# Roots of the mean squares: a row made by products with the identity, or by a store to DRAM and a load back

## The chip, the core and the metric

The program runs on one core of a Trainium2 chip. Such a core has five engines that each run their own list of instructions in order and wait for one another through semaphores: TensorE (PE, matrix products; its weight loads are listed as PEld), VectorE (DVE), ScalarE (ACT), GpSimd (POOL) and SyncE (SP), which here only issues DMAs. The metric is the device time of one execution in microseconds, the median of some runs. Profile times are from one profiled execution.

## The reference

The reference is two blocks of two layers each on one sequence of 256 tokens with 1024 channels, all in float32. Each layer is a feed-forward part, a mixer (attention of several kinds in the first block; a state-space scan and latent attention in the second), and a second feed-forward part. So there are eight feed-forward parts and four mixers, one after the other. What the change touches is the norm ahead of a feed-forward part:

```
def rmsnorm(x, g):
    xf = x.astype(jnp.float32)
    y = xf * lax.rsqrt(jnp.mean(xf * xf, axis=-1, keepdims=True) + EPS)
    return y.astype(x.dtype) * g

def swiglu(h, w_gate, w_up, w_down):
    return (jax.nn.silu(h @ w_gate) * (h @ w_up)) @ w_down

x = x + 0.5 * swiglu(rmsnorm(x, g), w_gate, w_up, w_down)      # w_gate, w_up: 1024 x 2816; w_down: 2816 x 1024
```

The root `rsqrt(...)` is one number for each token, 256 in all. As it scales whole rows of `x`, the kernel multiplies with the gains `g` first, does the products with `w_gate` and `w_up` on the unscaled rows, and scales the results by the roots afterwards.

## The kernel before

**Phases.** `PHASES` lists twelve phases; `T0[p]` is the number of the first weight tile of phase p. A feed-forward phase (`tensor_ffn`, `scalar_ffn`, `vector_ffn`) goes over 33 weight tiles of 1 MB: gate tile i and up tile i in turn for i = 0 to 10 (steps s = 0 to 21), then 11 tiles of `w_down`. Step s works on tile `T0[p] + s`.

**A weight tile's way.** SyncE loads it into one of three buffers `ST` (`load_tile`, L153 in the profile). ScalarE copies it to `WH` in the reduced precision fp32r (`weights_hi`, L117), VectorE takes the remainder `WL = ST - WH` (`weights_lo`, L120), and TensorE multiplies with both, so that a product has nearly the precision of float32. ScalarE and VectorE prepare tile `T0[p] + s + 2` in step s. SyncE loads tile i once VectorE has done with tile i - 3, which is in the same buffer. SyncE's list is written tile by tile in `sync_program`: small loads are placed behind a given tile's load, and whatever one of them waits for holds back all loads after it.

**A gate or up tile on TensorE.** For each of 8 slices k of the 1024 channels there are two products with `WH` (moving 512 columns, the high and low part of X beside each other) and two with `WL` (256 columns). The results lie the other way round from X: channels of the hidden layer are on the partitions, the 256 tokens are along the free axis. The four halves of the product for a gate tile use PSUM banks 4 and 5, those of an up tile 6 and 7. Before TensorE starts the next tile of the same kind, VectorE must have read the banks: ScalarE copies one half to `EB` and VectorE adds it to the other (`gate_sum` writes `GS` for a gate tile; the sum of an up tile goes to `HQ`, shown as `H`).

**The roots.** ScalarE squares and sums the rows of X (`rms`), and takes the square root; VectorE inverts it in step 1 (`rms_end`, the RECIPROCAL of L138), which gives `RR`, two columns of 128 partitions (`RR` is a part of the tile `SM`, and is shown as `SM`). In `RR` a token is a partition, but for the products a token is a position along the free axis, the same on all partitions. So a row `RBC` of 256 roots is wanted in each of the 128 partitions. `r_row`, after the products of step 2, makes it on TensorE: two float32 products of the identity (`ident`, a part of `C`) with one column of `RR` repeated 128 times, into bank 3. `row_end` copies the bank to `RBC` on VectorE at the end of its step 2. In step 3 VectorE multiplies `GS` by `RBC` (name `gg`), ScalarE takes its silu, and then VectorE multiplies `HQ` by `RBC` (`scale_up`) and by `GS`. These two products with `RBC` occur for each of the 11 pairs of tiles of a phase; the row is made once in a phase, and first used in step 3, ahead of the sum of gate tile 1 (`gate_sum`) that frees banks 4 and 5 for step 4.

The second block's mixers (`mix2`) also make a row with `r_row` and `row_end`.

Of the kernel before, what the change touches and what calls it, by code (L numbers as in the profile page):

```python
# [5 lines left out]
F32 = mybir.dt.float32  # L6
# [6 lines left out]
T, DM, DF = 256, 1024, 2816  # L13
# [327 lines left out]
def build(nc, I, consts, out, phases=PHASES):  # L341
# [3 lines left out]
    def sem(name):  # L345
        return ctx.enter_context(nc.semaphore(name))
# [11 lines left out]
    def at(*name):  # L358

        return known[name] if known else (PE.sem, 1)  # L360
# [21 lines left out]
    def ar(name, shape, off, dt=F32):  # L382
        return sb(name, shape, dt, ARENA + off)
# [62 lines left out]
    WS, DCOL, BROW = ar("WS", [128, 32], D0 + 512), ar("DCOL", [128, 16], D0 + 640), ar("BROW", [128, 3, 32], D0 + 704)  # L446
    QKR = ar("QKR", [128, 2, 64], D0 + 1088)
    AHT = ar("AHT", [32, T], D0 + 1600)
    SCR = nc.dram_tensor("decay", (2, 32, T), F32, kind="Internal").ap()
    CB = ar("CB", [128, 2, 2, 260], 80896)  # L450
    QNT, QRT = sb("QNT", [128, 2, 2, T], F32R, R2), sb("QRT", [128, 2, 2, T], F32R, R2 + 16384)
# [119 lines left out]
    s_gain, s_x = sem("gains_landed"), [sem("x0_landed"), sem("x1_landed")]  # L571
    s_ident, s_const, s_out = sem("ident_landed"), sem("const_landed"), sem("out_stored")
    s_par = [sem(f"par{l}_landed") for l in range(2)]
    s_scr = [sem(f"decay{l}_stored") for l in range(2)]
    s_dec = [[sem(f"decay{l}_half{n}_landed") for n in range(8)] for l in range(2)]
    landed, rounds = {}, [0] * NS
# [104 lines left out]
    def r_row(e, p, b):  # L681
        clear(b)
        e.wait_ge(*at("rr", p))
        for t in range(2):
            m = e.matmul(PS[:, b, of(t)], RR[:, t:t + 1].to_broadcast([128, 128]), ident, True, True)
        m.then_inc(*e.done("rrow", p))
        freed[b] = ("rbc", p)
# [22 lines left out]
    def tensor_ffn(e, p):  # L710
        begun = set()
        for s, (what, i) in enumerate(FFN):
            tile = T0[p] + s
            wh, wl = view(WH, tile), view(WL, tile)
            if tile not in CUT:
                e.wait_ge(*at("lo", tile))
            if what == "d":
                if i < NP - 2:
                    for name, a, kind, c in EIGHT if i in PLAIN else SEVEN:
                        ends = i == SUMMED[-1] and name in ("m1", "m5", "m6", "m7")  # L720
                        m = tensor_product(e, p, i, name, a, kind, c, begun, ends)
                        if ends:
                            m.then_inc(*e.done(name, p))
                    m.then_inc(*e.done("tile", tile))
                elif i == NP - 2:
                    freed.update({0: ("um", p), 1: ("x", p, 1, 1), 2: ("x", p, 0, 1), 3: ("x", p, 1, 0), 4: ("x5", p),
                                  5: ("x7", p), 6: ("um", p), 7: ("x", p, 0, 0)})
                    for group in ("m2", "m3", "c22", "m4"):
                        own = [(j, r) for j in (i, i + 1) for r in (EIGHT if j in PLAIN else SEVEN) if r[0] == group]
                        for j, (name, a, kind, c) in own:  # L730
                            if (group, j, c) == ("m4", i + 1, 1):
                                m.then_inc(*e.done("tile", tile))
                                if p + 1 < len(phases):
                                    turn_x(e, p + 1, "", 0)
                            m = tensor_product(e, p, j, name, a, kind, c, begun, (j, (name, a, kind, c)) == own[-1])
                        m.then_inc(*e.done(group, p))
                    e.also("tile", tile + 1)
                continue
            if p == 0 and s == 18:
                e.wait_ge(s_const, NCONSTS)  # L740
                for gi in range(1, 4):
                    turn_gains(e, gi, gi - 1)
            b = 4 + 2 * (what == "u")
            clear(b, b + 1)
            for k in range(8):
                if s == 0 and k == 3:
                    turn_x(e, p, "", 1)
                if tile in CUT:
                    e.wait_ge(*at("lo", tile, k * CUT[tile] // 8))
                if s == 0:  # L750
                    e.wait_ge(*at("xl", p, "", k))
                for f in range(2):
                    e.matmul(PS[:, b + f, :], wh[:, k, of(f)], XHL[:, k, :, :].rearrange("p a t -> p (a t)"), k == 0, False)
                for f in range(2):
                    m = e.matmul(PS[:, b + f, 0:256], wl[:, k, of(f)], XH[:, k, :], False, k == 7)
            m.then_inc(*e.done("tile", tile))
            freed[b] = freed[b + 1] = ("us" if what == "u" else "gs", p, i)
            if s == 2:
                r_row(e, p, 3)

    def wide(e, tile, hi, lo, ks, banks, first, last, cols, off=0):

# [873 lines left out]
    def row_end(e, p, b):  # L1636
        e.wait_ge(*at("rrow", p))
        e.wait_ge(*e.last())
        e.tensor_copy(RBC[:, :], PS[:, b, 0:256]).then_inc(*e.done("rbc", p))
# [66 lines left out]
    def scale_up(e, p, i):  # L1706

        h = HQ[i].rearrange("p (k t) -> p k t", k=2)
        e.wait_ge(*at("us", p, i))
        e.wait_ge(*at("rbc", p))  # L1710
        e.tensor_tensor(h, h, RBC[:, :].unsqueeze(1).to_broadcast([128, 2, T]), ALU.mult).then_inc(*e.done("un", p, i))

    def pair_sums(e, p, i):
# [37 lines left out]
    def vector_ffn(e, p):  # L1751
        t0 = T0[p]
        for s in range(len(FFN)):
            for i in range(NP):
                if s == UP_AT[i] + 1:
                    e.wait_ge(*at("ub", p, i))
                    e.tensor_tensor(HQ[i], PS[:, 6:8, 0:256], EB[:, :, :], ALU.add).then_inc(*e.done("us", p, i))
                if s == max(UP_AT[i] + 1, 3):
                    e.wait_ge(*at("rbc", p))
                    e.wait_ge(*at("gs", p, i))  # L1760
                    e.tensor_tensor(GS[i % 2], GS[i % 2], RBC[:, :].unsqueeze(1).to_broadcast([128, 2, T]),
                                    ALU.mult).then_inc(*e.done("gg", p, i))
                if s == GATE_AT[i] + 1 and (p or i):
                    gate_sum(e, p, i)
# [11 lines left out]
                tile_sums(e, p, s + 2 - DOWN)  # L1776
            if s == 1:
                rms_end(e, p)
            if s == 2:
                row_end(e, p, 3)  # L1780
            for i in range(NP):
                if s == HIDDEN_AT[i]:
                    e.wait_ge(*at("silu", p, i))
# [718 lines left out]
    def load_params(e, l):  # L2502
        for j, name in enumerate(("dt_bias_2", "a_log_2", "d_skip_2")):
            e.dma_start(BROW[:, j, :], I[name][l].unsqueeze(0).to_broadcast([128, 32])).then_inc(s_par[l], 16)
        for j, name in enumerate(("q_norm_2", "k_norm_2")):
            e.dma_start(QKR[:, j, :], I[name][l, 128:192].unsqueeze(0).to_broadcast([128, 64])).then_inc(s_par[l], 16)

    def load_decay(e, p, l, n):

        i = n  # L2510
        if n == 0:
            e.wait_ge(*at("ahl", p))
            e.dma_start(SCR[l], AHT[:, :]).then_inc(s_scr[l], 16)
            e.wait_ge(s_scr[l], 16)
            e.wait_ge(*at("ol", p, 7))
        if n == 2:
            e.wait_ge(*at("tile", T0[p] + MIX2T.index(("mla", 1)) + 1))
        if n > 3:
            e.wait_ge(*at("yo", p, 2 * HAD[n] + 1))
        e.dma_start(ME[i].rearrange("p h c t -> p (h c t)"), SCR[l, 4 * n:4 * n + 4, :].rearrange("h t -> (h t)").unsqueeze(0)  # L2520
                    .to_broadcast([128, 4 * T])).then_inc(s_dec[l][n], 16)
        for h in range(2):
            e.dma_start(EA[i][64 * h:64 * h + 64, :, :], SCR[l, 4 * n + h:4 * n + 4:2, 128:256].unsqueeze(0)
                        .to_broadcast([64, 2, 128])).then_inc(s_dec[l][n], 16)

    def sync_program(e):
        load_x(e, 0)
        e.dma_start(C[:, 0:128], consts[:, 0:128]).then_inc(s_ident, 16)
        load_rows(e, 0, *groups[0][0], s_gain)
        for j in range(CUT[0]):  # L2530
            load_part(e, 0, j)
            if j == 1:
                load_x(e, 1)
        for j in range(CUT[1]):
            load_part(e, 1, j)
        load_tile(e, 2)
        for i in range(NS, NT):
            load_tile(e, i)
            for j in range(2 * (i - NS), 2 * (i - NS) + 2):
                if j < NCONSTS // 16:  # L2540
                    load_const(e, j)
            for p, (kind, l, _) in enumerate(phases):
                if kind == "mix2" and i == T0[p] + 4:
                    e.wait_ge(*at("x", p - 1, 0, 1))
                    load_params(e, l)
                for n in range(8):
                    if kind == "mix2" and i == T0[p] + (30, 30, 35, 35, 36, 37, 40, 42)[n]:
                        load_decay(e, p, l, n)
        p = len(phases) - 1
        for t, n in ((1, 1), (1, 0), (0, 0), (0, 1)):  # L2550
            e.wait_ge(*at("x", p, t, n))
            e.dma_start(out[0, of(t), half(n)], X[:, t, half(n)]).then_inc(s_out, 16)
        e.wait_ge(s_out, 64)
# [63 lines left out]
```

## Time and profile before

| | |
|---|---|
| median of 3 runs | 2609.53 us (2609.23 to 2610.02) |
| profiled execution | 2610.11 us, of which 2608.3 us are the span from the first to the last instruction |
| TensorE matmul | busy 2593.6 us, 99% of the span, 14500 records |
| VectorE | busy 2080.4 us, 80% |
| ScalarE | busy 1550.4 us, 59% |
| DMA | 471.89 MB, queue 1 busy for 54.5% of 16 engines' span |
| TensorE's granted clock | 1.00 of full speed, the mean of the core |

A row of a timeline gives the start, the duration, the engine, the line, the operation with its output and input tiles, and the number of merged instructions; in brackets stands how long the engine sat idle before it, and who released it. The line is often that of a helper (L111 is any matmul, L120 any VectorE operation on two tensors, L153 any DMA), so the tile names tell the groups apart. Records of matmuls overlap: an instruction is pipelined behind the one ahead of it, and the distance between two starts is what it costs. A float32 product leaves two records in the trace.

### The profile page before, as it was taken

To read this page: it belongs to the slowest core of one execution; us is meant where nothing else is said; L and a number is where in the kernel's file an instruction comes from. 1 tells how busy PE (TensorE), PEld (TensorE's weight loads), DVE (VectorE), ACT (ScalarE), POOL (GpSimd) and SP (SyncE) were. 2 spreads that over 40 slices of the span, in tenths; PEclk is the share of its full clock that TensorE was granted. 3 is DMA by queue.
4 is the path that set the end of the run, shared out by engine and by line. 5 is a ranking of instruction groups with operands and counts; after the bars stand their busy time and mean duration, and the time that the engine had idled before them with its cause. 6 is when DMAs were issued, how large, how long until landed. Compare 5 with 4: busy or idle time off the path is not lost.

```text
span 2608.3 us, 35583 instructions
## 1 busy us (share of the span) xinstructions
PE 2593.6 (99%) x14500; PEld 2223.6 (85%) x14500; DVE 2080.4 (80%) x2647; ACT 1550.4 (59%) x2014; POOL 286.6 (11%) x254
## 2 busy tenths in 40 slices
PE   9999999999999999999999999999999999999999
PEld 7888788888888888888889998888888899988887
DVE  7897767887886767887888878678878888786788
ACT  6546665546556665545557767455455577674553
POOL 0003210000004110000003123200000031232000
PEclk9999999999999999999999999999999999999999
DMA  7554445555555445555555465555555564645553
GB/s 252 179 199 162 162 162 183 188 193 190 183 181 185 147 172 182 192 179 194 183 184 188 133 212 161 187 184 188 184 194 179 185 188 136 211 161 183 188 186 137
DMA packets 342752, 471.89 MB, mean 181 GB/s; under 512 B 18810, under 2 KB 259516, under 8 KB 342588
## 3 DMA queue, kind: packets, MB, share of 16 engines
q1 hardware_dynamic: 342588, 469.61, 54.5%
q8 instruction: 114, 1.87, 0.3%
q14 instruction: 50, 0.41, 0.0%
HBM read 468.46 MB, written 1.11 MB: 180 GB/s over the span
## 4 chain that ended last, share of the span: by engine, by line
PE 97%; DVE 1%; ACT 1%; issue 0%; DMA 0%; SPq 0%; DVEq 0%
PE PS L111 95%; PE PS L114 3%; DVE WL L120 1%; ACT WH L117 0%; ACT XHL L117 0%; DVE SB L125 0%; DMA ST<-in_ffn_w_gate 0%; DVE XB L128 0%; DVE H L120 0%; DVE ANG L125 0%; DVE ANG L128 0%; DVE XHL L128 0%; DVE SB L131 0%; ACT KV L117 0%; SPq L153 0%
## 5 line engine op out<-in xcount | busy, mean ns | idle before, releaser
L120 DVE TENSOR_TENSOR WL<-ST,WH 128x2048 fp32r<-128x2048 f32 (+3 forms) x442 | 988.4, 2236 | 209.2 <-ACT WH L117 205.4
L111 PE MATMUL PS<-XHL,WH 128*128 128x512 f32 (+1 forms) x4096 | 1123.5, 362 | 3.7 <-DVE XHL L128 2.3
L117 ACT ACTIVATE WH<-ST 128x2048 fp32r<-128x2048 f32 (+3 forms) x442 | 817.4, 1852 | 291.5 <-PE PS L111 285.4
L111 PEld LDWEIGHTS PS<-XHL,WL 128*128 128x128 f32 x3456 | 652.2, 189 | 125.3
L111 PE MATMUL PS<-XHL,WL 128*128 128x256 f32 x3456 | 735.1, 279 | 0.0
L111 PEld LDWEIGHTS PS<-XHL,WH 128*128 128x128 f32 x4096 | 629.2, 190 | 8.3 <-DVE XHL L128 3.3
L111 PE MATMUL PS<-WH,XHL 128*128 128x512 f32 (+3 forms) x1472 | 460.4, 387 | 0.0
L117 ACT ACTIVATE EB<-PS 128x512 f32<-128x512 f32 x176 | 105.3, 598 | 415.7 <-PE PS L111 412.6
L111 PEld LDWEIGHTS PS<-WH,XHL 128*128 128x128 f32 x1472 | 273.7, 188 | 58.2 <-issue 6.8
L111 PE MATMUL PS<-WL,XHL 128*128 128x512 f32 (+3 forms) x736 | 280.5, 381 | 0.0
L111 PE MATMUL PS<-WH,HH 128*128 128x512 f32 x544 | 215.1, 395 | 0.0
L111 PE MATMUL PS<-WH,HL 128*128 128x512 f32 x544 | 214.9, 395 | 0.0
L111 PE MATMUL PS<-WL,HH 128*128 128x512 f32 x544 | 214.0, 393 | 0.0
L120 POOL TENSOR_TENSOR X<-X,TS 128x512 f32<-128x512 f32 x8 | 14.4, 1797 | 1590.1 <-DVE TS L128 1590.1
L111 PEld LDWEIGHTS PS<-WL,XHL 128*128 128x128 f32 x736 | 138.5, 188 | 24.8 <-issue 1.0
L111 PE MATMUL PS<-WH,RH 128*128 128x512 f32 (+1 forms) x352 | 135.2, 384 | 1.2 <-ACT KV L117 1.2
L111 PE MATMUL PS<-WL,RH 128*128 128x512 f32 (+1 forms) x352 | 133.7, 380 | 0.0
L111 PE MATMUL PS<-WH,RL 128*128 128x512 f32 (+1 forms) x352 | 133.7, 380 | 0.0
L120 DVE TENSOR_TENSOR H<-PS,EB 128x512 f32<-128x512 f32 x88 | 60.8, 691 | 91.1 <-ACT EB L117 91.0
L111 PEld LDWEIGHTS PS<-WH,HL 128*128 128x128 f32 x544 | 102.1, 188 | 24.3
L111 PEld LDWEIGHTS PS<-WL,HH 128*128 128x128 f32 x544 | 102.1, 188 | 23.9
L111 PEld LDWEIGHTS PS<-WH,HH 128*128 128x128 f32 x544 | 102.2, 188 | 23.1
(274 smaller groups left out, 2954.6 us busy)
## 6 DMA issues: line engine op xcount, KB each, us to landing
ST<-in_ffn_w SPq DMA_DIRECT2D x132, 1024.0 KB, 4.9
ST<-in_w_in SPq DMA_DIRECT2D x106, 1024.0 KB, 5.1
ST<-in_ffn_w_down SPq DMA_DIRECT2D x44, 1024.0 KB, 4.9
ST<-in_ffn_w_gate SPq DMA_DIRECT2D x43, 1024.0 KB, 5.2
ST<-in_ffn_w_up SPq DMA_DIRECT2D x43, 1024.0 KB, 5.1
ST<-in_w_ssd_out SPq DMA_DIRECT2D x16, 1024.0 KB, 5.0
ST<-in_w_branch SPq DMA_DIRECT2D x8, 1024.0 KB, 5.0
ST<-in_w_out SPq DMA_DIRECT2D x8, 1024.0 KB, 5.1
```

The source lines that it names most:

```text
L111: return self.eng.matmul(o, l, r, start=start, stop=stop) if self.eng else Said()
L114: return self.eng.transpose(o, v, ident) if self.eng else Said()
L117: return self.eng.activation(o, v, f, **kw) if self.eng else Said()
L120: return self.eng.tensor_tensor(o, a, b, op) if self.eng else Said()
```

## The change

Only the eight feed-forward phases change. TensorE no longer runs `r_row` there, VectorE no longer runs `row_end`, and SyncE gets a new function `spread_roots`, placed directly behind the load of tile `T0[p] + 5`. It waits for the reciprocal `rr`, stores the two columns of `RR` to a DRAM tensor `ROOTS` (128 words of 4 bytes each), waits until both have landed, and loads the 256 words as a row into all 128 partitions of `RBC` (1 KB each). The two uses of `RBC` wait for the semaphore `s_row` of that load. The mixers keep their products with the identity.

```
+    ROOTS = nc.dram_tensor("roots", (len(phases), 2, 128), F32, kind="Internal").ap()
...
+    s_root, s_row = sem("roots_stored"), sem("roots_landed")
+
+    NTH = {p: sum(k == "ffn" for k, _, _ in phases[:p + 1]) for p in range(len(phases)) if phases[p][0] == "ffn"}
...
             freed[b] = freed[b + 1] = ("us" if what == "u" else "gs", p, i)
-            if s == 2:
-                r_row(e, p, 3)
...
         e.wait_ge(*at("us", p, i))
-        e.wait_ge(*at("rbc", p))
+        e.wait_ge(s_row, 16 * NTH[p])
...
                 if s == max(UP_AT[i] + 1, 3):
-                    e.wait_ge(*at("rbc", p))
+                    e.wait_ge(s_row, 16 * NTH[p])
...
-            if s == 2:
-                row_end(e, p, 3)
...
+    def spread_roots(e, p):
+
+        e.wait_ge(*at("rr", p))
+        for t in range(2):
+            e.dma_start(ROOTS[p, t].unsqueeze(1), RR[:, t:t + 1]).then_inc(s_root, 16)
+        e.wait_ge(s_root, 32 * NTH[p])
+        e.dma_start(RBC[:, :], ROOTS[p].rearrange("t p -> (t p)").unsqueeze(0).to_broadcast([128, T])).then_inc(s_row, 16)
...
+                if kind == "ffn" and i == T0[p] + 5:
+                    spread_roots(e, p)
```

TensorE, between step 2 and step 3 of a feed-forward phase (here the second such phase; the six others and the first read alike). `PS<-XHL,WH` and `PS<-XHL,WL` are the products of a tile, `PS<-C,SM` those with the identity:

```order
 L111 MATMUL PS<-XHL,WH 128x512 x2
 L111 MATMUL PS<-XHL,WL 128x256 x2
-L111 MATMUL PS<-C,SM 128x128 [waits dve_done]
-L111 MATMUL PS<-C,SM 128x128
 L111 MATMUL PS<-XHL,WH 128x512 [waits dve_done]
 L111 MATMUL PS<-XHL,WH 128x512
```

Two float32 products and one wait are gone, and nothing else moves on TensorE.

VectorE, at the end of step 2 and in step 3 of the same phase (`GS_73` is the buffer of gate tile 0, `GS_74` that of gate tile 1, `H_0_76` that of up tile 0):

```order
 L120 TENSOR_TENSOR H_0_76<-PS,EB 128x512 [waits act_done]
 L120 TENSOR_TENSOR WL<-ST,WH 128x2048 [waits act_done]
-L135 COPY RBC<-PS 128x256 [waits dve_done,pe_done]
-L120 TENSOR_TENSOR GS_73<-GS_73,RBC 128x512 [waits dve_done]
+L120 TENSOR_TENSOR GS_73<-GS_73,RBC 128x512 [waits roots_landed]
 L120 TENSOR_TENSOR GS_74<-PS,EB 128x512 [waits dve_done,act_done]
 L120 TENSOR_TENSOR WL<-ST,WH 128x2048 [waits act_done]
```

The copy is gone with its wait for TensorE; the first product with `RBC` now waits for a DMA, with the sum of gate tile 1 behind it.

SyncE, in the changed kernel, from the load of tile `T0[p] + 4` of the same phase on (`roots<-SM` are the stores, `RBC<-roots` is the load of the row; before, the five loads of `ST` follow one another):

```order
L153 DMA ST<-in_ffn_w_gate 128x8x256 [waits dve_done]
L153 DMA ST<-in_ffn_w_up 128x8x256 [waits dve_done]
L153 DMA roots<-SM 128x1 [waits dve_done]
L153 DMA roots<-SM 128x1
L153 DMA RBC<-roots 128x256 [waits roots_stored]
L153 DMA ST<-in_ffn_w_gate 128x8x256
L153 DMA ST<-in_ffn_w_up 128x8x256 [waits dve_done]
L153 DMA ST<-in_ffn_w_gate 128x8x256 [waits dve_done]
```

The load of tile `T0[p] + 6` now stands behind two waits: for the reciprocal and for the landing of the stores.

## Rows read from the trace of the kernel before

**Rows 1.** The page's busy times and the chain that ended last.
```profile
PE 2593.6 (99%) x14500; PEld 2223.6 (85%) x14500; DVE 2080.4 (80%) x2647; ACT 1550.4 (59%) x2014; POOL 286.6 (11%) x254
...
PE 97%; DVE 1%; ACT 1%; issue 0%; DMA 0%; SPq 0%; DVEq 0%
```

**Rows 2.** Timeline of TensorE around the row's products, the phase at 411 us.
```profile
424.58 0.63 PE L111 MATMUL PS<-XHL,WH 128*128 128x512 f32 x2
...
425.27 0.61 PE L111 MATMUL PS<-C,SM 128*128 128x128 f32 x4
425.64 0.71 PE L111 MATMUL PS<-XHL,WH 128*128 128x512 f32 x2
...
426.42 0.63 PE L111 MATMUL PS<-XHL,WH 128*128 128x512 f32 x2
...
431.30 0.63 PE L111 MATMUL PS<-XHL,WH 128*128 128x512 f32 x2
```

**Rows 3.** Instructions of tile SM: the row's products; ns min/median/max, first and last start.
```profile
L111 PE MATMUL PS<-C,SM x40: 270/275/275, 28.3 to 2440.4; 128*128 128x128 f32 x40
```

**Rows 4.** Timeline of VectorE, same phase, steps 1 to 3.
```profile
420.51 0.17 DVE L138 RECIPROCAL SM<-SM 128x2 f32<-128x2 f32 x1
...
422.33 2.29 DVE L120 TENSOR_TENSOR WL<-ST,WH 128x2048 fp32r<-128x2048 f32 x1 [0.86 <-ACT WH L117]
425.92 0.42 DVE L135 COPY RBC<-PS 128x256 f32<-128x256 f32 x1 [1.29 <-PE PS L111]
426.38 0.69 DVE L120 TENSOR_TENSOR GS<-GS,RBC 128x512 f32<-128x512 f32 x1
427.18 0.69 DVE L120 TENSOR_TENSOR GS<-PS,EB 128x512 f32<-128x512 f32 x1
```

**Rows 5.** Timeline of SyncE's queue, same phase.
```profile
414.56 0.37 SPq L153 DMA_DIRECT2D ST<-in_ffn_w_up  x1
420.50 0.37 SPq L153 DMA_DIRECT2D ST<-in_ffn_w_gate  x1
424.65 0.37 SPq L153 DMA_DIRECT2D ST<-in_ffn_w_up  x1
```

**Rows 6.** DMA issues: KB each, median us to landing.
```profile
ST<-in_ffn_w_up SPq DMA_DIRECT2D x43, 1024.0 KB, 5.1
...
out<-X SPq DMA_DIRECT2D x4, 256.0 KB, 2.1
...
QKR<-in_k_norm SPq DMA_DIRECT2D x2, 32.0 KB, 5.2
decay<-AHT SPq DMA_DIRECT2D x2, 32.0 KB, 5.2
```

**Rows 7.** Timeline of SyncE's queue: two DMAs of one word for each partition.
```profile
61.99 1.06 SPq L153 DMA_DIRECT2D POS<-in_positions  x2
```

**Rows 8.** SyncE's waits: us in total, times, longest.
```profile
SPq L153 <- DMA decay<-AHT: 9.2, 2, 4.8
```

**Rows 9.** Timeline of ScalarE and VectorE, same phase: tile 6 is split.
```profile
431.99 1.91 ACT L117 ACTIVATE WH<-ST 128x2048 fp32r<-128x2048 f32 x1
...
433.93 2.29 DVE L120 TENSOR_TENSOR WL<-ST,WH 128x2048 fp32r<-128x2048 f32 x1 [0.52 <-ACT WH L117]
...
437.07 0.60 ACT L117 ACTIVATE EB<-PS 128x512 f32<-128x512 f32 x1 [2.66 <-PE PS L111]
...
442.64 0.60 ACT L117 ACTIVATE EB<-PS 128x512 f32<-128x512 f32 x1 [2.65 <-PE PS L111]
```

**Rows 10.** Timeline of TensorE and VectorE in the first phase.
```profile
25.66 0.17 DVE L138 RECIPROCAL SM<-SM 128x2 f32<-128x2 f32 x1 [1.37 <-ACT SM L117]
...
27.96 2.29 DVE L120 TENSOR_TENSOR WL<-ST,WH 128x2048 fp32r<-128x2048 f32 x1 [1.12 <-ACT WH L117]
...
28.67 0.70 PE L111 MATMUL PS<-XHL,WH 128*128 128x512 f32 x2
```

**Rows 11.** Waits, 103 to 130 us: total us, times, longest.
```profile
PE PS L111 <- DVE GS L120: 1.4, 1, 1.4
```

## The prediction, made before the changed kernel was run

> **What bounds the kernel now.** I read the page's busy times and its chain of waits first. TensorE is busy for 99% of the span, and 97% of the chain that ended last is its own work [rows 1]. So a microsecond taken out of TensorE's list is a microsecond gained, and a microsecond added elsewhere costs nothing until TensorE waits for it. The second view is TensorE's timeline around the two products that go. The start of each record there follows the one before at an even pace and no idle time is shown: TensorE doesn't wait at this place [rows 2]. The third is VectorE's timeline: it does wait, 1.29 us, for TensorE to reach the row's products, and copies the row afterwards [rows 4]. The fourth and fifth are the queue of SyncE and the DMAs' landing times [rows 5, 6], as the new work goes there.
>
> **What goes on TensorE.** A slice k of a tile begins every 0.70 us: from the WH pair at 425.64 one would expect the next at 426.34, but it starts at 426.42 since the row's products still occupy the array. From the WH pair at 424.58 to that at 426.42 there are 1.84 us, in which two slices take 1.39 (a slice at 0.70: the copies to EB after steps 4 and 5 are 442.64 - 437.07 = 5.57 apart, eight slices). The row costs 1.84 - 1.39 = 0.45 us [rows 2, 9]. The trace has 40 records of these products, four to a row: ten rows, of which two are the mixers' and stay [rows 3]. At the seven other feed-forward phases the same distance is 1.83 or 1.84 us, so eight give 8 x 0.45 = 3.6 us. Nothing else moves on TensorE, and bank 3 is not used again until the tiles of w_down, so the saving is whole.
>
> **What goes on VectorE.** A copy of 0.42 us and the wait of 1.29 us in seven phases [rows 4]. VectorE is not waited for here: the sum of gate tile 1 ends at 427.18 + 0.69 = 427.87, while TensorE wants its banks at 431.30 [rows 2, 4]. I cost this at nothing. What it does is to leave VectorE free at 422.33 + 2.29 = 424.62 for the first product with the row, which stood at 426.38.
>
> **What comes: the row's way.** The roots are there at 420.51 + 0.17 = 420.68 [rows 4]. The trace before shows no store of single words. For the issue, the nearest rows are loads of one word for each partition: two took 1.06 us in the queue [rows 7], 0.53 each, so the second store starts at about 421.2. For a landing, the nearest rows are 2.1 us (256 KB stored from X, with nothing ahead of it) and 5.2 us (the decay rows, 32 KB, issued right behind a 1 MB tile) [rows 6]. Which of them applies is read from the queue: tile 5's load was issued at 414.56 and lands 5.1 us later, at 419.7, and tile 6's now stands behind the stores [rows 5, 6]. The queue is empty, so I take 2.1: landed at 423.3. The row's load is 128 KB from DRAM; between the same 2.1 us and 5.2 us (QKR, a load of 32 KB into all partitions behind a tile) [rows 6] I take 2.2, the lower end for the same reason: landed at 425.6, or 4.9 us after the roots. The product starts 0.8 us earlier than before instead of later. The bounds of the two landings are 2.1 + 2.1 and 5.2 + 5.2.
>
> The Trainium skill, "DMA: Bandwidth & Descriptors", section on the anatomy of one DMA, gives a fixed cost of about 2.0 us for each DMA, most of it the confirmation of the write. By it the row would come at about 425.5, and the sum would be the same. The same section warns that this "can cause a surprisingly long delay especially when the write target is HBM"; the stores of X to the output, at 2.1 us, show no such delay [rows 6], and that of the decay rows has its 1 MB tile ahead of it. What it would do here is rival (a) below.
>
> **How late may the row be?** Behind the waiting product stands the sum that frees banks 4 and 5. From the start of the product to the end of the sum are 427.87 - 426.38 = 1.49 us [rows 4]. TensorE starts step 4 at 431.30 - 0.45 = 430.85 [rows 2], so the row may land until 429.36, which is 8.7 us after the roots. There are 3.8 us to spare. The first phase is tighter, as its square sums come late: roots at 25.83, VectorE free at 30.25, the row by my figures at 25.83 + 4.9 = 30.75, and TensorE's step 4 at 28.67 + 5.66 - 0.45 = 33.88 (5.66 is 431.30 - 425.64), so until 32.39 [rows 2, 10]. 1.6 us to spare there.
>
> **What SyncE's waits hold back.** The stores wait for the roots and the row's load for the stores; the load of tile 6 is behind both. It was issued at 420.50 [rows 5]; now it is at about 423.3 + 0.5 = 423.8, 3.3 us later. It lands at 428.9 to 429.3. ScalarE begins to split it at 431.99, so nothing waits [rows 9]. With more delay it would still have room: WL is done 4.23 us after the start of the split (433.93 + 2.29 - 431.99), and TensorE starts step 6 at about 442.4 - 0.45 = 442.0 (the EB copy of step 5's banks at 442.64 marks it), so the tile may land until 437.7 [rows 9]. Tile 7, wanted from SyncE at 424.65 [rows 5], is issued on time; its bytes queue behind those of tile 6, by some 3 us, and it is split only after the copy to EB at 437.07 [rows 9]. The cost is nothing, and even at 5.2 us for each landing tile 6 would be issued at 427.1 and land at 432.2. In the row of SyncE's waits one sees that such a wait is paid by the queue itself: it stood 4.8 us for the decay store [rows 8].
>
> The Trainium skill states this on the same page and in the same section as a rule: DMA engines do not wait on semaphores, any wait is made by the issuing sequencer. The trace agrees with its 4.8 us.
>
> **Sum.** -3.6 us on TensorE, nothing elsewhere: the profiled execution of 2610.11 us would be 2606.5. The median of the runs shown is 0.6 lower, 2609.53, which gives 2605.9.
>
> **Rivals.**
> (a) The row comes late in every phase, and the kernel gets slower: stores of single words, 4 bytes at a time, are confirmed slowly. For it speaks that no row shows such a store. Each microsecond past 8.7 us from the roots is one on TensorE in each of eight phases. With both landings at 5.2 the row comes at 421.2 + 10.4 + 0.1 = 431.7, 2.3 us late: 8 x 2.3 - 3.6 = +15, or 2624.6. It equals the time before at 9.1 us from the roots, and is 0.2% slower from 9.8. Against it: the empty queue.
>
> (b) Only the first phase is late, where 1.6 us are spare and small loads of constants share the queue: up to 2 us of stall, 2605.9 to 2607.9.
>
> (c) The weight tile is late. This needs SyncE to be held until 432.6, 12 us after the roots; each microsecond more then costs one in each phase, so one past it gives 2605.9 + 8 = 2613.9. Against it: even the upper bounds of (a) don't reach it.
>
> (d) What TensorE saves is given back at a place where it waits for another engine, as 1.4 us at 125 us [rows 11]: 2609.5. Against it: that chain starts from a bank that TensorE filled, so it moves with TensorE.
>
> (e) The saving is larger, since VectorE (80% busy) is relieved too: 0.46 us more in each phase (426.38 - 425.92), 2605.9 - 3.7 = 2602.2. For it speaks VectorE's share, against it that TensorE shows no wait for VectorE in these steps [rows 2].
>
> **Chances.** A measurement of this kernel can tell about 0.2%, 5.2 us, from no change. Forecast 2605.9: 0.78; its own range is 2605.3 to 2606.6 (0.40 to 0.50 us a phase and the spread of the runs). (a) 0.08, of it 0.07 over 5.2 us slower; (b) 0.03; (c) 0.01, slower too; (d) 0.02; (e) 0.08, faster than 0.2%. So faster 0.08, same 0.84, slower 0.08. The forecast's gain itself, 0.14%, falls within the 0.2%. The range 2604.6 to 2609.6 holds the forecast, (b) and (d), and leaves (a), (c) and (e) out.
>
> **What the profile after would show.** TensorE: no records C,SM at the eight places, and 1.39 us for the two slices across the step. VectorE: the first GS<-GS,RBC waits for the DMA of RBC, about 1 us idle, and starts some 4.9 us after the reciprocal. SyncE: the load of tile 6 about 3.3 us after the reciprocal's end, and no wait of ScalarE for ST there. If TensorE has idle time ahead of step 4's first product, (a) is right; ahead of step 6's, (c). The prediction would be wrong if the row takes more than 8.7 us.

## The result, and the profile after

| | before | after |
|---|---|---|
| median, runs | 2609.73 us (2609.23 to 2610.15, 5 runs) | 2667.57 us (2665.91 to 2667.84, 5 runs) |
| ratio | | 1.0219, 95% interval 1.0208 to 1.0230 |
| span of the profiled execution | 2608.3 us | 2665.8 us |
| mean granted clock of TensorE | 1.00 | 0.99 |

The changed kernel is slower by 58 us. The forecast was 2605.9 us, in a range of 2604.6 to 2609.6. Busy times and chain of the page, which answer to [rows 1]:

```profile
PE 2609.0 (98%) x14468; PEld 2234.5 (84%) x14468; DVE 2074.9 (78%) x2639; ACT 1552.8 (58%) x2014; POOL 286.9 (11%) x254
...
PE 90%; DMA 4%; ACT 3%; DVE 2%; issue 0%; SPq 0%; ACTq 0%; DVEq 0%
```

TensorE has 32 records fewer and yet is busy 15.4 us longer, and the span is 57.5 us longer: its idle time grew by 57.5 - 15.4 = 42.1 us. DMAs are now 4% of the chain. The waits of the whole execution (us in total, times, longest) say who it waited for, and who that one waited for:

```profile
DVE GS L120 <- DMA RBC<-roots: 76.9, 8, 11.1
...
PE PS L111 <- DVE GS L120: 42.8, 9, 7.6
```

Eight of the nine waits of TensorE are new; the ninth is that of [rows 11]. "Third phase" here and below is the third of the twelve, which is the second feed-forward phase; before the change it stands at 411 us. There the chain in order of time (start, duration) shows the two steps of the row's way:

```profile
430.40 7.24 DMA roots<-SM
...
437.66 6.30 DMA RBC<-roots
```

Timeline rows of VectorE, SyncE's queue, TensorE and ScalarE in the same stretch, which answer to [rows 2, 4, 5, 9]:

```profile
429.83 0.17 DVE L138 RECIPROCAL SM<-SM 128x2 f32<-128x2 f32 x1
...
430.02 0.82 SPq L153 DMA_DIRECT2D roots<-SM  x2
437.66 0.32 SPq L153 DMA_DIRECT2D RBC<-roots  x1
438.02 0.43 SPq L153 DMA_DIRECT2D ST<-in_ffn_w_gate  x1
...
443.98 0.69 DVE L120 TENSOR_TENSOR GS<-GS,RBC 128x512 f32<-128x512 f32 x1 [10.05 <-DMA RBC<-roots]
444.78 0.69 DVE L120 TENSOR_TENSOR GS<-PS,EB 128x512 f32<-128x512 f32 x1
...
445.62 1.19 PE L111 MATMUL PS<-XHL,WH 128*128 128x512 f32 x2 [5.30 <-DVE GS L120]
...
447.06 1.91 ACT L117 ACTIVATE WH<-ST 128x2048 fp32r<-128x2048 f32 x1 [0.90 <-DMA ST<-in_ffn_w_gate]
```

The roots are there at 430.00, the row at 443.96: 14.0 us where 4.9 were forecast. For most of the stores' 7.2 us no DMA engine moves a byte; the last two figures of this row are the DMA share and GB/s from 432.00 to 437.60:

```profile
432.00:437.60 5.60, 5.60 (x34) 4.86 (x32) 1.93 (x1) 2.80 (x3) 0.00 (x0) 1.00 0.00 0
```

So that time is spent on the confirmation of the writes, not on moving them. TensorE stands for 5.30 us ahead of step 4 until the sum of gate tile 1 has freed its banks. And then it is slow. Three stretches of TensorE (us, busy us and records, granted clock, DMA share, GB/s): the stall, the 6 us behind it, and the next 5.6:

```profile
439.92:445.62 5.70, 0.40 (x4) 0.91 0.62 214
445.62:451.58 5.96, 5.96 (x18) 0.52 0.94 296
451.58:457.20 5.62, 5.62 (x34) 1.00 0.79 241
```

The granted clock was 1.00 while TensorE worked. It fell within the 5.3 us of idle time (mean 0.91 over the stall), and over the next 6 us it is 0.52, that is 0.50 for most of them (1.2 GHz in place of 2.4): 18 records where the next stretch has 34. In the timeline a slice of a tile takes 1.28 us there in place of 0.70.

**The account.** Idle time +42.1 us. Busy time +15.4, which is -3.7 for the products that are gone (TensorE is busy 2589.9 us in the version without stalls, below) and +19.1 that are left for the slow clock, 2.4 a phase. 42.1 - 3.7 + 19.1 = 57.5 us. The clock itself bears the 19.1 out: over the 6.0 us behind each of the eight stalls its mean was 0.74, 0.52, 0.67, 0.56, 0.56, 0.59, 0.59 and 0.72, which makes 6.0 x 3.05 = 18.3 us of lost work, 1.6 to 2.9 in a phase. All eight new waits stand ahead of step 4. They make 41.4 of the 42.1 us, so no more than 0.7 us is idle time anywhere else, ahead of step 6 for one.

### The profile page after: what moved, and what is told of

Its sections match the earlier page's. It is cut to its first block, busy times and chain, and to the rows that moved or that the text cites. A ratio compares the mean times of both kernels' runs of the same rounds, so it can differ in the third digit from the quotient of the medians.

```text
span 2665.8 us, 35535 instructions
## 1 busy us (share of the span) xinstructions
PE 2609.0 (98%) x14468; PEld 2234.5 (84%) x14468; DVE 2074.9 (78%) x2639; ACT 1552.8 (58%) x2014; POOL 286.9 (11%) x254
## 2 busy tenths in 40 slices
DMA packets 346208, 472.94 MB, mean 177 GB/s; under 512 B 21242, under 2 KB 262972, under 8 KB 346044
## 4 chain that ended last, share of the span: by engine, by line
PE 90%; DMA 4%; ACT 3%; DVE 2%; issue 0%; SPq 0%; ACTq 0%; DVEq 0%
PE PS L111 87%; PE PS L114 3%; DMA roots<-SM 2%; DMA RBC<-roots 2%; ACT WH L117 1%; DVE WL L120 1%; ACT JK L117 1%; ACT XHL L117 1%; DVE GS L120 0%; ACT L117 0%; ACT EB L117 0%; DVE SB L125 0%; DMA ST<-in_ffn_w_gate 0%; DVE XB L128 0%; SPq L153 0%
## 5 line engine op out<-in xcount | busy, mean ns | idle before, releaser
L111 PE MATMUL PS<-XHL,WH 128*128 128x512 f32 (+1 forms) x4096 | 1136.4, 365 | 45.5 <-DVE GS L120 42.8
L111 PEld LDWEIGHTS PS<-XHL,WL 128*128 128x128 f32 x3456 | 660.0, 191 | 128.4
L111 PEld LDWEIGHTS PS<-XHL,WH 128*128 128x128 f32 x4096 | 636.6, 192 | 51.5 <-DVE GS L120 44.4
```

The source lines that it names most:

```text
L111: return self.eng.matmul(o, l, r, start=start, stop=stop) if self.eng else Said()
```

## Experiments

All start from the changed kernel unless said otherwise. Landing times are counted from the issue, as medians over the eight phases. All experiments but e9 are single runs; the kernel before varied from 2608.9 to 2610.4 us over its runs, so a difference in the whole time of 1 or 2 us from a single run says little, and the landing times carry the argument.

**1. What makes the store and the load slow?** Four kernels. In all four the row is loaded from fixed words of a weight matrix, and the stores vary:

```
e1   -e.dma_start(RBC[:, :], ROOTS[p].rearrange("t p -> (t p)").unsqueeze(0).to_broadcast([128, T]))
     +e.dma_start(RBC[:, :], I["w_in"][0, 0, 0:T].unsqueeze(0).to_broadcast([128, T]))
e2   e1, and ROOTS is (len(phases), 2, 128, 128); a word is stored to ROOTS[p, t, :, 0:1]
     (with allow_slow_non_contiguous=True on the stores, as in e11, e13 and e14 below)
e3   e1, and ROOTS as in e2; X[:, t, 0:128] is stored to ROOTS[p, t]
e4   e1, without the stores and the wait for them
```

> Leaves out the roots: the row is loaded from 256 words of a weight matrix in DRAM in place of the words just stored; stores and waits as in the changed kernel. There the stores landed about 6.8 us after issue and the row 6.2 us. Theory 'fresh' (the row is slow since it reads lines that were written a moment ago): row 2.2 us, idle of TensorE for the row down from 5.3 to about 1.3 us a phase, about 2626 us in all. Theory 'hot' (the row is slow since 128 partitions read the same 1 KB): row stays at 6.2 us, 2667 us in all. Both: stores unchanged at 6.8.

> As the run before (row from a weight matrix, roots left out), and each stored word goes to an address of its own 512 B from the next. Theory 'shared lines' (128 words in 512 B are written by 16 engines into the same few lines, one after the other): stores land in 2.1 to 2.5 us. Theory 'words' (a write of 4 B is slow to be confirmed wherever it goes): 6.8 us as before. If the stores take 2.1 us and the row 6.2, the row lands about 9.3 us after the roots and the kernel takes about 2612 us; if both are unchanged, 2667.

> As the runs before, and each partition stores 512 B (a piece of X, two times 128 x 512 B = 128 KB) in place of a word. Theories 'shared lines' and 'words': no small writes are left, so the stores land in 2.1 to 2.5 us like those of the output. Theory 'any store in the midst of the kernel is slow' (a small DMA that follows the 1 MB loads): 6 to 7 us. The row as in the two runs before.

> As the runs before, without any store: SyncE waits for the roots and loads the row from the weight matrix at once. Theory 'hot': row 6.2 us after its issue, 6.3 us after the roots, before the 8.7 us at which TensorE would have to wait; so no idle time of TensorE ahead of step 4 and 2606 us (the 3.6 us of the two products are gained). Theory 'fresh': row at 2.3 us, and also 2606 us. The landing time of the row tells them apart, the total doesn't.

DMA issues of the four (KB each, median us to landing), first e1:

```profile
RBC<-in_w_in SPq DMA_DIRECT2D x8, 128.0 KB, 5.1
roots<-SM SPq DMA_DIRECT2D x16, 0.5 KB, 6.5
```

e2, words 512 B apart:

```profile
RBC<-in_w_in SPq DMA_DIRECT2D x8, 128.0 KB, 5.1
roots<-SM SPq DMA_DIRECT2D x16, 0.5 KB, 1.5
```

e3, blocks of 512 B:

```profile
roots<-X SPq DMA_DIRECT2D x16, 64.0 KB, 1.6
RBC<-in_w_in SPq DMA_DIRECT2D x8, 128.0 KB, 4.9
```

e4, the row's load alone:

```profile
RBC<-in_w_in SPq DMA_DIRECT2D x8, 128.0 KB, 4.7
```

The store: the same 256 words take 6.5 us side by side and 1.5 us apart. So it is not that a write is of 4 B, nor a store in the midst of the loads, but where the words lie. The words aren't merged or split on the way either: e1 and e2 both have 346208 DMA packets, 21242 of them under 512 B. The load: the row of `ROOTS` took 6.2 us and a row of the weight matrix 5.1, but 4.7 us remain even with nothing ahead of it. That the extra 1.1 us comes from the words being just written isn't shown, as the two rows also lie in different places; the copies of e9 below are just written too and land in 2.4 us. In all: 2653.8, 2608.0, 2608.6 and 2607.1 us, against 2610.0 before. In the third phase of e2 the row comes 6.3 us after the roots, inside the 8.7 us of the prediction, and TensorE has one new wait, of 0.96 us in the first phase. There the row comes 7.52 us after the roots, and the prediction's limit was 32.39 - 25.83 = 6.56, so it is late by just this 0.96, as rival (b) had it. I expected 2612 for e2 since I had added up 9.3.

**2. How does the store's time go with distance and number?**

```
e11  e2 with ROOTS (len(phases), 2, 128, 16): 64 B apart
e13  ... (len(phases), 2, 128, 8): 32 B          e14  ... (len(phases), 2, 128, 2): 8 B
e15  e1 with "for t in range(1)": one column, 128 words side by side
```

> As the run with the words 512 B apart, at 64 B (row from a weight matrix, roots left out). Words that are 4 B apart landed 6.5 us after issue, words 512 B apart 1.5. If what counts is a line of 64 B or less, 1.5 us here; if it is a piece of 512 B of which several words fall into one (8 words in each), about 2 to 3 us.

> Words 32 B apart (row from a weight matrix, roots left out). At 4 B the stores landed 6.5 us after issue, at 64 B 1.5. If several words in one line of 64 B are what costs, two in each here: little more than 1.5, under 2.5. If all that matters is that two words touch, 1.5.

> Words 8 B apart (row from a weight matrix, roots left out). By shared lines of 64 B there are 8 words in a line, against 16 at 4 B: about half of the extra time, 1.5 + 2.5 = 4.0 us. If a line is 32 B or less, less; if the place matters in larger pieces (512 B), 5 us or more.

> Only one of the two columns is stored, 128 words 4 B apart in 512 B (row from a weight matrix, roots left out). If the writes queue behind each other line by line, each line has as many words as with two columns and the stores land after the same 6.5 us or a little less. If all words queue at one place whatever their line, half of the extra time: 4.0 us.

Measured: 1.5 us at 64 B, 1.5 at 32 B, 2.7 at 8 B, and with one column at 4 B 7.2 us. The rows of e15:

```profile
RBC<-in_w_in SPq DMA_DIRECT2D x8, 128.0 KB, 4.3
roots<-SM SPq DMA_DIRECT2D x8, 0.5 KB, 7.2
```

Half of the words don't take less time, so it is no queue of all words at one place; the words that lie close together hold one another up. (Each column has 512 B to itself in both, so the number of words within one such piece, 128, was never varied at 4 B.) From 8 B to 4 B the extra time goes from 1.2 to 5 us, not from 2.5 to 5 as I expected of lines of 64 B. How large the piece of DRAM is, by what mechanism its writes hold one another up, and why the growth is so steep, stays open. The totals were 2609.0, 2607.0, 2609.5 and 2642.9 us.

**3. How does the load's time go with the number of readers?**

```
e5   e4 with I["w_in"][0, 0:128, 0:T]: 128 different rows of 1 KB
```

> No stores; after the roots SyncE loads 128 different rows of 1 KB of a weight matrix into RBC, in place of one row of 1 KB into all partitions (roots left out). With the one row the load took 4.2 us in the third phase and 4.7 us at the median. Theory 'hot' (what makes it slow is that 128 reads go to the same 1 KB): 2.2 to 2.5 us at the third phase. Theory 'load' (any load of 128 KB takes that long here, as the 1 MB tile behind it shares the engines): 4.2 and 4.7 us again. In all about 2607 us by both.

```profile
RBC<-in_w_in SPq DMA_DIRECT2D x8, 128.0 KB, 2.2
```

The same 128 KB in pieces of 1 KB, at the same place in the queue, landed in 2.2 us when each partition reads its own row, and in 4.7 when all read one. The forecast's 2.2 us is the price of this load when it is not a broadcast. (2606.3 us in all, 2609.0 before.)

**4. The two halves of the change.** e6 takes the products and the copy away and loads a fixed row once at the start. e7 is the kernel before with `spread_roots` added, its row going to a place that nobody reads. (VectorE waits for its landing in step 10 and SyncE for that of the phase before; both waits show no time.)

```
e6   +                if p == 0 and i == T0[p] + 3:
     +                    fixed_row(e)                      # one load of RBC; VectorE waits for s_row >= 16
e7   +    RBD = ar("RBD", [128, T], 12288)
     ...
     +        e.dma_start(RBD[:, :], ROOTS[p].rearrange("t p -> (t p)").unsqueeze(0).to_broadcast([128, T])).then_inc(s_row, 16)
```

> The removed part alone: the products with the identity and the copy are gone in the eight phases, and no DMA is put in their place but one load of a fixed row at the start (roots left out). The records say 0.45 us for each phase, so 3.6 us less than before, 2606.3. The rival is that what VectorE is relieved of counts too: 2602.

> The added part alone: TensorE and VectorE make the row as before, and SyncE's stores, its wait and its load of the row are added as in the changed kernel, into a place that nobody reads. If only the lateness of the row costs, this takes as long as before, 2610. If the weight tile 6, held back behind the stores, costs too, it is slower: the tile landed 17 us after the roots in the changed kernel, where it may land until 17.0 by my sum, so up to 1 us a phase, 2618.

e6: 2606.6 us, with 2609.0 for the kernel before next to it; the profiled span is 3.5 us shorter than that of before, and TensorE is busy 4.1 us less. By single runs the removal is worth 2.4 to 4.1 us, which holds its 3.6; the eleven runs of e9 below say it better. e7: 2634.5 us, 25 us slower, though nobody stands still for the row. What comes late is weight tile 6. Its waits between 436 and 453 us:

```profile
DVE WL L120 <- ACT WH L117: 7.1, 1, 7.1
ACT WH L117 <- DMA ST<-in_ffn_w_gate: 6.5, 1, 6.5
...
PE PS L111 <- DVE GS L120: 2.5, 1, 2.5
```

ScalarE stands 6.5 us for the tile, at the head of its list; the silu of pair 1 and the copy to EB stand behind it, VectorE stands 7.1 us behind ScalarE, and the sum that frees banks 4 and 5 for step 6 is late by 2.5 us. So the tile's deadline isn't when its own products are due, but when what stands behind its split is due. In the whole execution TensorE's idle time is 17.0 us longer (span +24.4, busy +7.4).

The slow clock followed only three of its eight stalls. Behind those of 3.81, 2.43 and 2.01 us the clock's mean over 5.7 us was 0.55, 0.72 and 0.70; behind that of 2.50 us, in the third phase, it stayed at 1.00:

```profile
451.62:457.30 5.68, 5.68 (x33) 4.97 (x34) 5.68 (x5) 3.55 (x5) 0.00 (x0) 1.00 0.85 266
```

**5. Does the late tile add to the late row?** One move in the changed kernel: the load of tile 6 is issued between the stores and the wait for them.

```
+                if kind == "ffn" and i == T0[p] + 5:
+                    store_roots(e, p)
+                if kind == "ffn" and i == T0[p] + 6:
+                    spread_roots(e, p)                   # waits for the stores, loads the row
```

> The changed kernel with one move: the load of tile 6 is issued between the two stores and the wait for them. The row comes as late as before, 14 us after the roots; tile 6 is on time. If the row alone makes the changed kernel's 58 us (5.3 us of idle time a phase and the slow clock behind it), this takes 2665 to 2668 too. If the late tile adds to it behind the stall, up to 1 us a phase comes back: 2658.

It took 2681.5 us, 14 more than the changed kernel, outside both expectations. The tile was on time, but its 1 MB now went beside the stores, and both landings grew, the stores' from 6.7 us and the row's from 6.2 us; that the tile's bytes held them up is the likely reason and isn't shown by itself:

```profile
RBC<-roots SPq DMA_DIRECT2D x8, 128.0 KB, 6.6
roots<-SM SPq DMA_DIRECT2D x16, 0.5 KB, 7.7
```

In the third phase the row came 17.2 us after the roots in place of 14.0, and TensorE stood for 8.5 us. So the edit changed both quantities and doesn't answer the question by itself. It shows that the row's lateness goes to TensorE one to one: over the eight phases the rows came 16.4 us later than in the changed kernel, and the waits for GS are 59.1 us in all against 42.8, 16.3 more. The span grew by 13.8 only, as TensorE was busy 2.8 us less: longer stalls (5.5 to 9.4 us) had no more slow clock behind them (2606.2 - 2589.9 = 16.3 us against 19.1). For the question itself the trace of the changed kernel has the answer: none of its new waits stands ahead of step 6, so beside the late row the late tile cost next to nothing.

**6. The row without either collision.** VectorE copies the roots 16 times beside each other and transposes the tile in 32 x 32 blocks, so that a partition holds 32 roots in one piece of 128 B. The stores make 16 copies of the row in DRAM, and a copy is read by 8 partitions. Nothing is left out.

```
 rms_end(e, p)                     # waits and semaphores of the new lines are left out here
+e.tensor_copy(RR32[:, :].rearrange("p (c t) -> p c t", t=2), RR.unsqueeze(1).to_broadcast([128, 16, 2]))
+e.turn32(RT32[:, :], RR32[:, :])                        # VectorE's transpose of 32 x 32 blocks
...
+for b in range(4):
+    e.dma_start(ROOTS[p, :, :, 32 * b:32 * b + 32].rearrange("c t r -> (c t) r"), RT32[32 * b:32 * b + 32, :])
+e.wait_ge(s_root, 64 * NTH[p])
+e.dma_start(RBC[:, :], ROOTS[p].rearrange("c t r -> c (t r)").unsqueeze(1).to_broadcast([16, 8, T]))
```

> Nothing left out. VectorE copies the two columns of roots 16 times beside each other and transposes the tile in blocks of 32 x 32, so that each partition holds 32 roots one after the other; four stores of 32 x 128 B make 16 copies of the row in DRAM, and each copy is loaded by 8 partitions. Theory 'shared lines': no line is written twice, the stores land 1.5 to 2.1 us after issue. Theory 'hot': the load, with 16 source rows, takes less than 4.7 us, some 2.5. Then the row is there about 6.5 us after the roots, and the kernel takes 2606 to 2607 us. If the load still takes 5 to 6 us (sources just written), the row comes 9 to 10 us after the roots: up to 1.3 us of idle time a phase and its clock, 2610 to 2630.

> The turned version again (transposes on VectorE, 128 B per partition, 16 copies), timed against the kernel before: one run gave 2606.4, so 2606.3 +- 0.5, a ratio of 0.9987. The gain is the 8 x 0.45 us of TensorE, less what else moved.

> The turned version with the row's load from 4 of the 16 copies, each read by 32 partitions. Reading one copy by all 128 took 4.7 to 6.2 us, 16 copies 2.4, 128 different rows 2.2. If the reads of one place queue behind each other, the time grows with the readers of a copy: 2.2 + 32/128 x (4.7 to 6.2 - 2.2) = 2.8 to 3.2 us. In all 2606.5 us, as the row is still early enough.

The DMA issues of e9:

```profile
RBC<-roots SPq DMA_DIRECT2D x8, 128.0 KB, 2.4
roots<-RT SPq DMA_DIRECT2D x32, 4.0 KB, 1.4
```

And its waits, in the columns used above:

```profile
DVE GS L120 <- DMA RBC<-roots: 12.0, 8, 2.4
...
PE PS L111 <- DVE GS L120: 1.4, 1, 1.4
```

The stores land below the forecast's 2.1 us and the row near its 2.2 us, TensorE is left with the one wait that it had before, and the kernel takes 2606.5 us (11 runs) against 2610.0 (15 runs), a ratio of 0.9987 (0.9978 to 0.9996). The gain of 3.5 us is the 3.6 that the prediction gave to the change, small but clear of the noise, and the kernel is faster than both. e8, the same kernel in a single run, took 2606.4. With 4 copies read by 32 partitions each (e12) it took 2607.2 us, and VectorE's wait for the row grew:

```profile
DVE GS L120 <- DMA RBC<-roots: 23.1, 8, 4.1
```

That is 1.4 us more a phase, so a row in about 3.8 us, above the 2.8 to 3.2 expected. But e12 changed a second thing. Its load is shaped `[4, 32, T]` in place of `[16, 8, T]`, and in its trace the load's semaphore moves 5 times for each load, once 1 us after the issue and four times between 3.2 and 4.0 us; in e9 it moves 16 times, between 2.1 and 2.6 us. That fits a load carried by four of the 16 DMA engines, and an engine then has four times the bytes. So e12 doesn't price 32 readers. What is left is 2.2 us at 1 reader, 2.4 at 8, and 4.7 to 6.2 at 128; how the time grows in between is open.

## Why the prediction was wrong, point by point

- **What goes on TensorE: right.** Busy time fell by 3.7 us where there are no stalls, against 8 x 0.45 = 3.6, and e9 confirms it in the whole time with 3.5 us; e6, the removal alone in a single run, agrees. What VectorE was relieved of was worth nothing, so rival (e) was out.
- **What comes: the step that failed.** "The queue is empty, so I take 2.1: landed at 423.3", and 2.2 for the row. The queue was indeed empty, and the landings were 7.2 and 6.3 us in the third phase. The landing time of the nearest rows was read as a function of what is ahead in the queue and of bytes. It depended on addresses: 256 words stored side by side (6.5 us against 1.5 when apart), and one row of 1 KB read by 128 partitions (4.7 us against 2.2 for 128 rows). A hint of the second stood in the trace before: QKR, also a broadcast, at 5.2 us, was put down to the tile ahead of it alone [rows 6]. How much of its 5.2 us is the tile and how much the broadcast is not tested.
- **The bounds.** They were said to hold 5.2 + 5.2 and so +15 us. The two landings took 7.2 + 6.3. A bound taken from the nearest rows doesn't bound an operation that none of them resembles; stores of single words were named as never seen, and then bounded all the same.
- **How late may the row be: right.** The limit was 8.7 us after the roots, the row came at 14.0, and TensorE stood for 5.30 us. In the first phase the limit was 6.56, the row came at 14.12, and TensorE stood for 7.56.
- **Rival (a): the right outcome by half of the reason**, with a chance of 0.08 and a price of +15. The row was late in every phase, and the stores were confirmed slowly. But "stores of single words, 4 bytes at a time" aren't slow as such (1.5 us when apart), and it had no word for the slow broadcast. Its price lacked two things: the true landings, and the clock. TensorE worked at a granted clock of 0.50 for a while behind each stall: 19 of the 58 us.
- **What SyncE's waits hold back: wrong too, though it was hidden.** Tile 6 "may land until 437.7", 17.0 us after the roots, was taken from its own use. In e7 it landed 17.9 us after the roots and cost 2.5 us of idle time in the third phase, where by my limit it would have been about 0.4, and 25 us in all. The true limit in e7 was 17.9 - 2.5 = 15.4 us. Rival (c) missed it from the other side too: it took 5.1 us for the tile's landing and so let SyncE be held for 12 us after the roots, but in e7 the tile, behind the row's load in the queue, was issued at 435.81, 8.6 us after the roots, and took 9.3 us. In the changed kernel the tile was there 17.1 us after the roots, past that limit too, but the late row had already moved everything behind it by 5.3 us, and no wait ahead of step 6 is left.
- **The sentence of the Trainium skill** in "DMA: Bandwidth & Descriptors", section on the anatomy of one DMA, that confirmation of a write to HBM can take surprisingly long: the trace agrees, with 7.2 us for the stores and no byte moved from 432.0 to 437.6. But the same target confirms the same words in 1.5 us when they are 32 B or more apart. The prediction quoted the section's 2.0 us for each DMA; the page gives it for DMAs that GpSimd issues. The stores here, issued by SyncE, landed in 1.4 to 7.7 us. Its table of specifications says that transfers below 512 B are made as read-modify-write; writes of 4 B at 1.5 us show that this alone isn't slow.

## What to carry to other kernels

Before a small DMA is put on a path with a deadline, ask who else touches the same bytes: words from many partitions that lie 4 B apart in DRAM took over 4 times as long as the same words further apart (6.5 against 1.5 us), and a broadcast of one short row to 128 partitions over twice as long as 128 different rows (4.7 against 2.2). Transposing first and keeping some copies brought both back to 1.4 and 2.4 us. Give a queue's wait the deadline of everything behind it, on each engine that it reaches, and not that of the one transfer. And allow for more than its length when you price a stall of TensorE: here 1.6 to 2.9 us of slow clock came behind each stall of 3.9 to 7.6 us, and in e7 five of eight stalls had none behind them.

## What the runs showed that I had not expected

- 128 or 256 words of 4 B stored side by side from 128 partitions: 6.5 to 7.2 us to landing. At 8 B distance 2.7 us, at 32, 64 and 512 B 1.5 us. One column of 128 words took no less time than two columns.
- 128 KB loaded into 128 partitions: 2.2 us from 128 rows of 1 KB, 2.4 from 16 rows (just written, and read by 8 partitions each), 4.7 from one row of a weight matrix (4.2 to 5.1 in the other runs where it was loaded in each phase), 6.2 from the one row of `ROOTS`.
- Stores to DRAM behind an empty queue landed in 1.4 to 1.6 us (4 KB and 64 KB), quicker than the 2.1 us of the output's 256 KB.
- A stall of TensorE doesn't have a fixed price in clock: 1.6 to 2.9 us of lost work behind each of eight stalls of 3.9 to 7.6 us, 16.3 us in all behind eight longer ones (5.5 to 9.4 us, e10), and none behind five of the eight shorter ones of e7.
